# Splitting the input projections of a mixer into three fp32r passes, with a weight ring of three slots

## The reference

```python
for l in range(DEPTH):                      # DEPTH = 2
    mod = c_act @ ada_w[l] + ada_b[l]
    sh_m, sc_m, g_m, sh_f, sc_f, g_f = jnp.split(mod[:, None, :], 6, axis=-1)
    h = _rmsnorm(x, norm_mix[l]) * (1 + sc_m) + sh_m
    proj = h @ w_in[l]                      # 1024 -> all of the parts below
    qa, ka, va, cq, ckv, kr, z, xbc, dt_raw, gates = jnp.split(proj, _IN_OFFSETS, axis=-1)
    ...
    oa = _diff_attention(qa, ka, va, positions, rel_bias, lam)
    ...
    ob = _mla_attention(qb.transpose(0, 2, 1, 3), kb.transpose(0, 2, 1, 3), vb.transpose(0, 2, 1, 3))
    ...
    xbc = jax.nn.silu(_causal_dwconv(xbc, ssm_conv_w[l], ssm_conv_b[l]))
    ...
    ys = _ssd(xs, dt, a, bm, cm) + ssm_d[l].astype(f32)[:, None] * xs.astype(f32)
    ...
    ga, gb, gc = jnp.split(jax.nn.sigmoid(gates), 3, axis=-1)
    merged = ga * (ya @ w_branch_a[l]) + gb * (yb @ w_branch_b[l]) + gc * (ys @ w_branch_c[l])
    x = x + g_m * (merged @ w_out[l])
    ...                                     # then an FFN with a convolution of three taps
```

## Time and profile before

| | |
|---|---|
| time, median of 3 runs | 2522.3 us (2520.91 to 2523.94) |
| the profiled execution: time, span | 2522.31 us, 2520.5 us |
| busy: TensorE, VectorE, ScalarE, GpSimd | 94%, 58%, 41%, 2% |
| mean granted clock of TensorE | 0.962 of full |
| transfers | 390.11 MB, mean 155 GB/s |

### The profile page before, as it was taken

One profiled execution on the slowest core, in us unless ns is written; L12 is line 12 of the kernel. 1 busy time (PEld: TensorE's weight loads), 2 busy tenths in 40 slices (PEclk: granted clock), 3 DMA queues, 4 the chain that ended last, 5 costly groups with the idle time before them and its releaser, 6 DMA issues. The chain is left out here.

```text
span 2520.5 us, 36404 instructions
## 1 busy us (share of the span) xinstructions
PE 2362.7 (94%) x13590; PEld 1998.9 (79%) x13590; DVE 1469.7 (58%) x2785; ACT 1033.8 (41%) x1824; POOL 52.6 (2%) x73
## 2 busy tenths in 40 slices
PE   6999988999999999989999999978999999988998
PEld 3656777889976577778999899856998899856997
DVE  4796514166743572332766766763766766763765
ACT  2222333145533334231555554434554554444554
POOL 0000000100000000011000000000000000000000
PEclk9999999999999999999999999979999999979999
DMA  8654222345445522224554455212554455213551
GB/s 345 250 225 150 100 101 80 147 153 197 176 161 218 197 101 104 98 100 152 191 184 175 178 190 200 83 43 108 200 192 150 160 190 200 86 40 112 199 189 67
DMA packets 37535, 390.11 MB, mean 155 GB/s; under 512 B 4416, under 2 KB 5056, under 8 KB 5952
## 3 DMA queue, kind: packets, MB, share of 16 engines
q1 hardware_dynamic: 37440, 388.87, 41.7%
HBM read 387.80 MB, written 1.05 MB: 154 GB/s over the span
## 5 line engine op out<-in xcount | busy, mean ns | idle before, releaser
L1150 PE MATMUL bank<-h,ring 128*128 128x256 f32 x2048 | 478.0, 389 | 13.2 <-ACT h L986 8.1
L1150 PEld LDWEIGHTS bank<-h,ring 128*128 128x128 f32 x2048 | 390.1, 193 | 104.1 <-issue 27.6
L632 DVE TENSOR_TENSOR ffn_w_lo<-ring,ffn_w_hi 128x2048 fp32r<-128x2048 f32 x126 | 288.9, 2293 | 165.3 <-ACT ffn_w_hi L581 165.2
L502 PE MATMUL bank<-ffn_hh,ffn_w_hi 128*128 128x512 f32 x1408 | 363.4, 399 | 13.3 <-DVE ffn_hh L762 9.0
L502 PEld LDWEIGHTS bank<-ffn_hh,ffn_w_hi 128*128 128x128 f32 x1408 | 257.7, 192 | 66.8 <-issue 9.4
L554 PE MATMUL bank<-ffn_g_hi,ffn_w_hi 128*128 128x256 f32 x1056 | 299.3, 283 | 6.2 <-DVE ffn_g_lo L677 6.1
L554 PE MATMUL bank<-ffn_g_lo,ffn_w_hi 128*128 128x256 f32 x1056 | 298.8, 283 | 0.0
L554 PE MATMUL bank<-ffn_g_hi,ffn_w_lo 128*128 128x256 f32 x1056 | 298.8, 283 | 0.0
L581 ACT ACTIVATE ffn_w_hi<-ring 128x2048 fp32r<-128x2048 f32 x126 | 240.6, 1910 | 1.3
L554 PEld LDWEIGHTS bank<-ffn_g_hi,ffn_w_hi 128*128 128x128 f32 x1056 | 202.7, 192 | 7.4 <-issue 7.4
L554 PEld LDWEIGHTS bank<-ffn_g_hi,ffn_w_lo 128*128 128x128 f32 x1056 | 202.7, 192 | 0.0
...
## 6 DMA issues: line engine op xcount, KB each, us to landing
ring<-w_in SPq DMA_DIRECT2D x244, 1536.0 KB, 6.4
...
```

The costliest lines, as they stand in the source:

```text
L502: pe.matmul(up_out(j, half, False), w_hi[:, j % 2, c0:c0 + P], hh[:, k, :, :], start=k == 0, stop=False)
L632: dve.tensor_tensor(w_lo[:, j % 2, UP], ring[:, (base + j) % RING, UP], w_hi[:, j % 2, UP], ALU.subtract).then_inc(S(tag + "_up_lo"), 1)
L1150: m = pe.matmul(ps[0:m_rows, 0:T], tile(t0 + k, base)[:, 0:m_rows], rhs, start=k == 0, stop=k == len(src) - 1 and kind != "uk")
```

## The change

- 102 blocks take the three-pass form: in layer 0 `xbc2` to `xbc15` and all 24 gates (38 blocks), in layer 1 all 64 blocks. Eight fp32 matmuls become 24 fp32r matmuls of the same size: `h_hi` with the high weights, `h_lo` with the high weights, `h_hi` with the low weights.
- A new step `wsplit` for each such block stands ahead of the `proj` two blocks earlier (AHEAD = 2; two buffers each of `w_high` and `w_low`). ScalarE copies the block's 128x1024 of the ring to `w_high`, once the block before in this buffer has been multiplied and the slot is there; VectorE subtracts for `w_low`.
- `h` is split too. In layer 0 by a step `hsplit` after the last early block and ahead of `vt`: ScalarE copies eight 128x256 to `h_hi`, VectorE subtracts eight for `h_lo`. In layer 1 ScalarE's shift writes `h_hi` at once, in place of `h`, and VectorE makes `h_lo` from the scaled `h`, the shift and `h_hi`.
- In layer 1 four `ada` chunks (HEAD_CHUNKS) stand between `start` and the first block. The few instructions on lambda (`lam`) move from `start` to ahead of block `krdt`.
- The new buffers take the place of one ring slot: RING is 3, and the loops over the FFN's slots on ScalarE and VectorE take six slots a round (TURN) in place of four. Work buffers of the mixer are laid over each other more tightly (not shown).

```diff
-RING = 4
+RING = 3
+TURN = RING if RING % 2 == 0 else 2 * RING
...
+    head = HEAD_CHUNKS if layer else 0
+    chunks_first, chunks = [s for c in chunks[:head] for s in c], chunks[head:]
+    steps.insert(steps.index(("proj", "krdt", 0)), ("lam", "", 0))
...
-        out = [("start", "", 0)] + out
-    return (out + [("pad", "", 4), ("vt", "va", 0), ("vt", "va", 1), ("vt", "vb", 0), ("vt", "vb", 1)]
+        out = [("start", "", 0)] + chunks_first + [("first", "", 0)] + out
+    return (out + ([("hsplit", "", 0), ("first", "", 0)] if layer == 0 else []) + [("pad", "", 4), ("vt", "va", 0), ("vt", "va", 1), ("vt", "vb", 0), ("vt", "vb", 1)]
...
+HEAD_CHUNKS = 4
+AHEAD = 2
+DEEP = ("cq", "ckv", "krdt", "qk", "va", "z", "xbc", "gate")
+
+
+def split_blocks(layer, steps):
+
+    late = lambda s: s[1] == "gate" or s[1] == "xbc" and s[2] >= XBC_EARLY
+    return [s[1:] for s in steps if s[0] == "proj" and s[1] in DEEP and (layer or late(s))]
+
+
+def with_splits(steps, blocks):
+
+    out = []
+    for s in steps:
+        if s[0] == "first":
+            out += [("wsplit", *b) for b in blocks[:AHEAD]]
+            continue
+        if s[0] == "proj" and s[1:] in blocks and blocks.index(s[1:]) + AHEAD < len(blocks):
+            out.append(("wsplit", *blocks[blocks.index(s[1:]) + AHEAD]))
+        out.append(s)
+    return out
...
+        a = steps1a(layer)
+        self.split = split_blocks(layer, a + STEPS1B)
+        self.a, self.b = with_splits(a, self.split), with_splits(STEPS1B, self.split)
...
+            if deep:
+                for name, shape in (("h_hi", [P, KD, T]), ("h_lo", [P, KD, T]), ("w_high", [P, AHEAD, UNIT]),
+                                    ("w_low", [P, AHEAD, UNIT])):
+                    work[name] = phase.enter_context(nc.sbuf_tensor(f"{name}{phases['n']}", shape, F32R))
...
-                            fetch(sp, 3)
+                            for g in range(3, RING):
+                                fetch(sp, g)
...
-                    act.activation(h[:, j, :], h[:, j, :], ACT.Identity, bias=mod[:, j:j + 1]).then_inc(S("m_h"), 1)
-
-                act.wait_ge(S("lam_dots"), 1)
-                act.activation(lamc[:, 2:4], lamc[:, 0:2], ACT.Exp).then_inc(S("lam_exp"), 1)
+                    if layer == 0:
+                        act.activation(h[:, j, :], h[:, j, :], ACT.Identity,
+                                       bias=mod[:, j:j + 1]).then_inc(S("m_h"), 1)
+                    else:
+                        act.activation(h_hi[:, j, :], h[:, j, :], ACT.Identity,
+                                       bias=mod[:, j:j + 1]).then_inc(S("h_high"), 1)
...
+                if layer:
+                    for k in range(KD):
+                        dve.wait_ge(S("h_high"), k + 1)
+                        dve.scalar_tensor_tensor(h_lo[:, k, :], h[:, k, :], mod[:, k:k + 1], h_hi[:, k, :], ALU.add,
+                                                 ALU.subtract).then_inc(S("h_low"), 1)
...
+            def split_weights_high(act, b):
+
+                n = fb.index(b)
+                if n >= AHEAD:
+                    act.wait_ge(S("tiles_used"), USED1[fb[n - AHEAD]][0])
+                for g, c0, cols, at in pieces(TILES1[b], base):
+                    act.wait_ge(full[g % RING], 16 * (g // RING + 1))
+                    act.activation(w_high[:, n % AHEAD, at:at + cols], ring[:, g % RING, c0:c0 + cols],
+                                   ACT.Copy).then_inc(S("w_high"), 1)
+
+            def split_weights_low(dve, b):
+
+                n = fb.index(b)
+                for i, (g, c0, cols, at) in enumerate(pieces(TILES1[b], base)):
+                    dve.wait_ge(S("w_high"), pieces_before[n] + i + 1)
+                    dve.tensor_tensor(w_low[:, n % AHEAD, at:at + cols], ring[:, g % RING, c0:c0 + cols],
+                                      w_high[:, n % AHEAD, at:at + cols], ALU.subtract).then_inc(S("w_low"), 1)
+
+            def split_block_pe(pe, b, ps, m_rows):
+
+                n, t0 = fb.index(b), TILES1[b][0]
+                pe.wait_ge(S("w_high"), pieces_before[n + 1])
+                for p_, (low, rhs) in enumerate(((False, h_hi), (False, h_lo), (True, h_hi))):
+                    if p_ == 2:
+                        pe.wait_ge(S("w_low"), pieces_before[n + 1])
+                    for k in range(KD):
+                        if n == 0 and p_ < 2:
+                            pe.wait_ge(S("h_low" if p_ else "h_high"), k + 1)
+                        w_ = (w_low if low else w_high)[:, n % AHEAD, k * P:k * P + P]
+                        m = pe.matmul(ps[0:m_rows, 0:T], w_[:, 0:m_rows], rhs[:, k, :], start=p_ == 0 and k == 0,
+                                      stop=p_ == 2 and k == KD - 1)
+                m.then_inc(S("tiles_used"), USED1[b][1])
...
+                    elif step == "hsplit":
+                        for k in range(KD):
+                            act.activation(h_hi[:, k, :], h[:, k, :], ACT.Copy).then_inc(S("h_high"), 1)
+                    elif step == "wsplit":
+                        split_weights_high(act, (kind, j))
...
+                        dve.wait_ge(S("tiles_used"), USED1["xbc", XBC_EARLY - 1][0])
+                        for k in range(KD):
+                            dve.wait_ge(S("h_high"), k + 1)
+                            dve.tensor_tensor(h_lo[:, k, :], h[:, k, :], h_hi[:, k, :],
+                                              ALU.subtract).then_inc(S("h_low"), 1)
+                    elif step == "wsplit":
+                        split_weights_low(dve, (kind, j))
```

91 lines of the change are left out of this document (59 added, 32 removed).

## The result

The changed kernel takes 2580.68 us (median of 4 runs, 2576.26 to 2585.68), the kernel before beside it 2521.61 (4 runs): a ratio of 1.0236, 95% interval 1.022 to 1.0253. Forecast were 2528 and a range up to 2542. The sign was right and nearly all of the size was missed: +59.1 us for +5.8.

The account below looks back on a forecast made before the run. The prediction took TensorE, 94% busy, as the bound only in places, with VectorE's and ScalarE's added work lengthening attention and the mixer's second half. Its gains and losses summed to +5.8 us on 2522.3, so 2528, range 2508 to 2542.

Parts of the forecast that it names:

- Ceiling and prices: All 102 blocks: 0.57 us saved each, 58.1 us if only TensorE counts; each adds a 1.05 us copy and 1.22 us subtraction.
- Entries to attention: Before the first scores: ScalarE's added copies stand ahead of the vt copies, +4.6 us in layer 0, +1.05 in layer 1.
- Attention with convolutions: Stretch of attention that also convolves: single-block units go from 5.05 to 5.5 us, +3.6 us a layer, clock apart.
- The units with two blocks: Three units in attention with convolutions, about 8.5 us each: VectorE would need 8.5 us, so no change.
- by totals: Cross-check for attention with convolutions: VectorE needs 64.3 of 66.20 us, leaving 1.9 for waits, so the stretch should grow.
- The clock: Attention with convolutions: longer waits cost one more loss of TensorE's clock, +1.5 us a layer, +3.0 for both.
- Gates in attention: Attention's stretch with gate blocks only: eight blocks save 4.6 us, one wait costs 1.1, so -3.5 us a layer.
- Layer 1 ahead of attention: 26 blocks before layer 1's attention: 14.8 us saved, +2 for later releases and copies ahead of evacuations, so -12.8 us.
- rival 3: Layer 1's first part: copies ahead of evacuations hold TensorE's banks, +13 us over the sum, 2541; chance 0.22.
- Layer 1's start: Start of layer 1: four ada chunks fill TensorE's wait, the first block starts about 3.8 us later; cancelling to 0.
- Ring of three: One ring slot fewer: late slots at the very start, +1.6 us, and among layer 0's chunks, +3.1; together +4.7.
- Second halves: Second half of each mixer: late dt delays the first cb by 4.4 us, later blocks give some back; +2.5 us a layer.

Follow-up runs that it names:

- evac_first: The changed kernel with each split one place later, behind the block's evacuation and convolution, no work taken away; 2564.08 us.
- low_late: The changed kernel with attention's weight copies behind the block's evacuation and the subtractions between a softmax and its probabilities; 2568.09 us.
- conv_fp32: The changed kernel with xbc2 to xbc15 left in fp32 in both layers, 28 blocks, so 74 blocks split; 2548.28 us.
- near_slot: The changed kernel with each split no earlier than where its tiles lie in the ring slot in use or the next; 2561.97 us.
- ring3: The kernel before with one edit, a ring of three slots in place of four; 2517.66 us against 2522.67, ratio 0.9991.
- dt_first: The changed kernel with the step on dt ahead of gate8 and gate9 in the second half of the mixer; 2578.64 us.

## Why the prediction was wrong

- **Ceiling and prices**: right. 2.88 us a block at full clock, 1.05 and 1.22 us for copy and subtraction.
- **Entries to attention**: right, +5.1 and +1.1 for +4.6 and +1.05.
- **Attention with convolutions**: the failing step is "the chain from one block's end is: ScalarE copies the weights of two blocks on". I let the chain begin at the end of TensorE's block and had two blocks' time for it, 11.0 us, so 5.5 a unit. ScalarE's queue has the exponential in front of the copy. The order rows show that (ScalarE's rows 97 to 99 at the entry), and I used them only for the entry. The length that I gave the chain, 6.2 us, was right; but it closes on itself, and it is passed once a unit and not once in two. The units with two blocks, put at no change, grew too (from 7.9 us to 9.3 and 9.8). So +3.6 a layer was +15.5 and +12.8, together with the clock. evac_first, which takes the copy out of the chain, brings layer 1's unit to 5.5 us; low_late, which takes out the subtraction as well, to 5.1 to 5.3 where nothing else waits; conv_fp32 removes the loss. The sum "by totals" (VectorE 64.3 of 66.2) misled too: VectorE was busy for 60.42 us, and the stretch was 23 us longer than that.
- **The clock**: +1.5 a layer was near: about 2 us in layer 0 and nothing visible in layer 1. The granted clock fell far more than I had thought (0.83 and 0.90), but mostly where TensorE had time to spare.
- **Gates in attention**: -3.5 was taken from TensorE's work, 8 x 0.57 less one wait. TensorE instead waits for VectorE's probabilities at three turns, 1.36, 1.69 and 1.94 us, where it waited 0.75 once before, and this eats the 4.6. No run took the splits of these blocks away alone. At the last of the three turns a copy that waits for a block, and its subtraction, stand in front of the probabilities:

```profile
340.48 1.06 ACT L1156 ACTIVATE w_high<-ring 128x1024 fp32r<-128x1024 f32 x1 [1.55 <-PE bank L1178]
...
341.57 1.22 DVE L1164 TENSOR_TENSOR w_low<-ring,w_high 128x1024 fp32r<-128x1024 f32 x1 [1.66 <-ACT w_high L1156]
...
343.51 0.55 PE L1298 MATMUL bank<-con,work 128*128 128x128 f32 x3 [1.94 <-DVE work L1582]
```
- **Layer 1 ahead of attention**: the failing term is "+2 ... an estimate between 0 and 10". I priced the copy as a delay of an evacuation and left out what it waits for. My rival 3 had the place and a price of +13 over the sum; the truth was 22 over, by a wait for slots that I had looked at in the section on the ring for TensorE only. There I asked when a slot is first multiplied. With splits the first user is ScalarE, up to three slots earlier. near_slot shows it. A first part that doesn't shrink was also the sign that I had named for rival 3.
- **Layer 1's start**: 0 was forecast, +4.3 measured. The block waits for `w_high` 3.50 us behind the chunks, starts at half clock (755.85), and the next slots are late.
- **Ring of three**: both places were right. TensorE waits 6.39 us for the slot at 26.0 (4.69 before, +1.6 forecast) and 2.94 for the one at 136.28 (+3.1 forecast). But of the +4.7 only +2.7 is left at the first `vt`, and nothing on the whole (ring3).
- **Second halves**: +3.6 and +4.2 measured for +2.5 each, not by `dt` (dt_first), and by the copies as far as the rows tell.
- **The range** held one mechanism of this kind at a time. Two of them, the chain in attention and the wait for slots, shared a cause, work put into an in-order queue with a wait of its own, and came together.
